# Block 0 of each feed-forward layer computed token-major, one tile of 128 tokens after the other

## The chip, the cores and the metric

One NeuronCore of a Trainium2 chip runs the whole program. The metric is device time in microseconds (us) of one launch; lower is better.

## The reference

Two small transformer stacks, two layers each, follow each other on one activation `x` of 256 tokens by 1024 features, batch 1, in fp32. Every layer ends in a gated feed-forward:

```python
x = x + swiglu(rmsnorm(x, norm_ffn[layer]), w_gate_up[layer], w_down[layer])    # first stack
h = rms_norm(x, ffn_norm[l])                                                      # second stack
x = x + (jax.nn.silu(h @ w_gate[l]) * (h @ w_up[l])) @ w_down[l]
```

Ahead of the four feed-forwards stand, in this order: a pooling mixer, a blockwise attention (called moba in the kernel), and twice a mixer of four attentions (called mix). The hidden width is 2816; each of the attention stages ends with an output projection whose product is added to `x`.

## The kernel before

**Precision by splitting.** Every large product is made of three: a weight is stored as `whi` (ACT copies `raw` to fp32r) plus `wlo` (DVE subtracts `whi` from `raw`), the activation as `h_hi` plus `h_lo`, and hi*hi, hi*lo and lo*hi are summed in PSUM. One **unit** is 1 MB of weights, 128 partitions by 2048. `split` on ACT makes `whi` (L619), `split` on DVE makes `wlo` (L904). There are 179 units in one fixed sequence, three slots each for `raw`, `whi` and `wlo`; a slot is free for ACT when PE has used unit n-3, and the load of a unit (SP, L412) waits until the low part of unit n-3 is made. The counters are semaphores: `hi_ready`, `lo_ready`, `units_used`.

**The order of work** is written out by hand for each engine; nothing is scheduled by a planner. Each engine executes its own list from top to bottom, and a wait stops all that stands behind it on that engine. The two attention stages are lists of events (`moba_script`, `mix_script`) that PE, ACT and DVE each walk through.

**Attention's end.** The output projection takes four units. `residual` (L1365 to L1367) multiplies one unit of 2 x 128 rows of weights into four accumulators, PSUM banks 4 to 7 (`ACC`): token tile t and column half h go to `ACC[2t+h]`, with 6 matmuls of 512 columns each, so 24 per unit. Before, each unit is done for both tiles before the next one begins.

**The norm.** For tile t, DVE adds each accumulator to `x` (`add_residual`, L914), ACT squares with a sum (L630), DVE adds up (L920), GpSimd (POOL) takes the power -0.5 (L568), DVE scales (`normalise`, L932), PE transposes eight 128x128 pieces (L1474, banks 0 to 3), ACT copies them as `h_hi` (L637) and DVE makes `h_lo` (L939). Before, DVE's `norm` does both tiles' adds first, and PE waits for all four halves ahead of block 0.

**The feed-forward** (`ffn(f)`, f = 0 to 3; its first unit is u0). The hidden width is cut into 11 blocks of 256; a block has three units, gate, up and down. Gate and up are computed feature-major: the weights stand still and the tokens stream, in two parts of 512 and 256 columns (`both_halves`, L1391 and L1395, 32 matmuls a unit). The two kinds of sum lie side by side in PSUM, and DVE adds them (`sum_gate`, L1029; `sum_up`, L1036). The first unit of block 0 is special, `first_both_halves` (L1406, L1407, L1410, then L1391 and L1395): it starts as soon as `h_hi` is there. Then ACT's silu (L669) and DVE's product and split (`glu`, L1044, L1051, L1053) give `o_hi` and `o_lo` for the down unit, which is done one block later. PE's order is gate 0, up 0, gate 1, up 1, down 0, gate 2, up 2, down 1 and so on. The end of a feed-forward is already computed by tile: the last two down units are done for tile 0 first, then for tile 1, and for f = 0 and f = 2 `residual` puts the eight transposes of the next norm's tile 0 between the halves of tile 1. The stage behind it then begins token-major (`first_token_major`, L1435, L1436, L1439), with tile 1's transposes between the tiles.

## Time and profile before

| | |
|---|---|
| median of 3 runs | 1178.37 us (1177.03 to 1178.8) |
| the profiled execution | 1178.07 us, of which its span 1176.0 us |
| matmuls (PE), DVE, ACT busy | 97%, 67%, 46% of the span |
| DMA | 205 MB, 174 GB/s, 54.4% of 16 engines' span |
| TensorE clock granted, mean | 0.991 of full |

The rows of a timeline give the start in us from the span's beginning, the length in us, engine, source line and operation, output and inputs; in square brackets, how long the engine sat idle before it and what released it. `x16` means sixteen in a row that were merged. Matmuls are pipelined: a row says 0.39 us for one, but the next one starts 0.23 us later, so rates are read from starts.

### The profile page before, as it was taken

How to read it: one execution, taken by the hardware profiler on the slowest of the kernel's cores; microseconds unless marked ns; L12 is line 12 of the kernel's file. 1: busy time of each engine (PE TensorE's matmuls, PEld its weight loads, DVE VectorE, ACT ScalarE, POOL GpSimd, SP SyncE). 2: the span in 40 equal slices, each digit the busy share in tenths (PEclk: the TensorE clock that was granted, in tenths of full speed). 3: DMA queues.
4: the chain of work that ended last, by engine and by line, in shares of the span. 5: the costliest groups of instructions: out<-in, count | busy, mean ns of one | idle time of the engine just before them, and what ended most of it. 6: DMA issues, size and time to landing. Idle time of an engine off the chain costs nothing.

```text
span 1176.0 us, 17176 instructions
## 1 busy us (share of the span) xinstructions
PE 1139.4 (97%) x6750; PEld 989.8 (84%) x6750; DVE 789.1 (67%) x997; ACT 535.5 (46%) x696; POOL 34.7 (3%) x47
## 2 busy tenths in 40 slices
PE   6899999999999999999999999999999999999997
PEld 4788888899878888889988788888898887888886
DVE  4776666856667666677676676666766766766665
ACT  4534333456654343344566433433446655333332
POOL 0000000000000000002100000000030000000000
PEclk9899999999999999999999999999999999999999
DMA  8565656673436556586432465565863234655560
GB/s 276 195 215 179 213 179 185 208 244 115 141 117 227 179 179 213 179 219 197 152 107 86 139 224 182 183 206 181 217 202 112 73 112 139 206 188 182 185 204 36
DMA packets 167672, 205.14 MB, mean 174 GB/s; under 512 B 19983, under 2 KB 150535, under 8 KB 167618
## 3 DMA queue, kind: packets, MB, share of 16 engines
q1 hardware_dynamic: 167618, 204.40, 54.4%
q8 instruction: 37, 0.61, 0.2%
q14 instruction: 17, 0.14, 0.0%
HBM read 203.22 MB, written 1.16 MB: 174 GB/s over the span
## 4 chain that ended last, share of the span: by engine, by line
PE 90%; DVE 3%; SPq 2%; ACT 1%; issue 1%; POOL 1%; DMA 0%; DVEq 0%; POOLq 0%; ACTq 0%
PE bank L1391 27%; PE bank L1395 14%; PE bank L1365 13%; PE bank L1366 13%; PE bank L1367 13%; PE bank L1582 3%; PE bank L1594 2%; PE bank L1474 1%; PE bank L1604 1%; ACT junk L630 1%; PE bank L1798 1%; DVE x L914 1%; PE bank L1741 1%; DVE xn L932 1%; POOL rstd L568 1%
## 5 line engine op out<-in xcount | busy, mean ns | idle before, releaser
L619 ACT ACTIVATE whi<-raw 128x2048 fp32r<-128x2048 f32 x177 | 338.6, 1914 | 413.7 <-PE bank L1395 271.0
L904 DVE TENSOR_TENSOR wlo<-raw,whi 128x2048 fp32r<-128x2048 f32 x176 | 403.5, 2294 | 162.4 <-ACT whi L619 162.3
L1391 PE MATMUL bank<-h_both,whi 128*128 128x512 f32 x1376 | 327.6, 390 | 0.0
L1391 PEld LDWEIGHTS bank<-h_both,whi 128*128 128x128 f32 x1376 | 255.0, 188 | 50.8
L1395 PEld LDWEIGHTS bank<-h_both,wlo 128*128 128x128 f32 x1376 | 176.7, 191 | 6.9
L1395 PE MATMUL bank<-h_both,wlo 128*128 128x256 f32 x1376 | 178.8, 283 | 0.0
L1365 PE MATMUL bank<-whi,o_hi 128*128 128x512 f32 x448 | 175.9, 393 | 0.6 <-DVE o_lo L1142 0.6
L1366 PE MATMUL bank<-wlo,o_hi 128*128 128x512 f32 x448 | 174.9, 390 | 0.0
L1367 PE MATMUL bank<-whi,o_lo 128*128 128x512 f32 x448 | 174.4, 389 | 0.0
L1365 PEld LDWEIGHTS bank<-whi,o_hi 128*128 128x128 f32 x448 | 84.3, 188 | 18.4 <-issue 2.3
L1367 PEld LDWEIGHTS bank<-whi,o_lo 128*128 128x128 f32 x448 | 84.1, 188 | 17.9
L1366 PEld LDWEIGHTS bank<-wlo,o_hi 128*128 128x128 f32 x448 | 84.3, 188 | 15.6
L1029 DVE TENSOR_REDUCE pr<-bank 128x512 f32<-128x1024 f32 x44 | 53.9, 1224 | 49.0 <-PE bank L1395 49.0
L1365 PE MATMUL bank<-h_both,whi 128*128 128x256 f32 x288 | 83.3, 289 | 0.0
L1366 PE MATMUL bank<-h_both,whi 128*128 128x256 f32 x288 | 81.5, 283 | 0.0
L1367 PE MATMUL bank<-h_both,wlo 128*128 128x256 f32 x288 | 81.4, 283 | 0.0
L1036 DVE TENSOR_REDUCE pr<-bank 128x512 f32<-128x1024 f32 x40 | 49.0, 1224 | 46.2 <-PE bank L1395 46.2
L703 ACT ACTIVATE pr<-pr,negmax 128x256 f32<-128x256 f32 (+1 forms) x96 | 46.0, 480 | 31.1 <-DVE negmax L1118 31.1
L1365 PEld LDWEIGHTS bank<-h_both,whi 128*128 128x128 f32 x288 | 55.1, 191 | 2.6 <-issue 2.3
L1366 PEld LDWEIGHTS bank<-h_both,whi 128*128 128x128 f32 x288 | 55.2, 192 | 0.1
L1367 PEld LDWEIGHTS bank<-h_both,wlo 128*128 128x128 f32 x288 | 55.2, 192 | 0.0
L1365 PE MATMUL bank<-whi,h_both 128*128 128x256 f32 x160 | 46.4, 290 | 1.5 <-DVE wlo L904 1.5
(165 smaller groups left out, 1144.2 us busy)
## 6 DMA issues: line engine op xcount, KB each, us to landing
raw<-in_w_gate_up SPq DMA_DIRECT2D x44, 1024.0 KB, 5.1
raw<-in_w_down SPq DMA_DIRECT2D x44, 1024.0 KB, 4.9
raw<-in_w_gate SPq DMA_DIRECT2D x22, 1024.0 KB, 5.3
raw<-in_w_up SPq DMA_DIRECT2D x22, 1024.0 KB, 5.3
raw<-in_w_in SPq DMA_DIRECT2D x20, 1024.0 KB, 6.3
raw<-in_w_o SPq DMA_DIRECT2D x12, 1024.0 KB, 5.0
raw<-in_w_kv SPq DMA_DIRECT2D x8, 1024.0 KB, 5.6
raw<-in_w_q SPq DMA_DIRECT2D x4, 1024.0 KB, 6.2
```

The costliest lines, as they stand in the source:

```text
L619: act.activation(whi[:, s, :], raw[:, s, :], ACT.Copy).then_inc(hi_ready, 1)
L703: e = act.activation(pr[:, s, q, 0:w], src, ACT.Exp, bias=negmax[:, s, q:q + 1], scale=-1.0 if biased else 1.0, accum_out=psumrow[:, s, q: ...
L904: dve.tensor_tensor(wlo[:, s, :], raw[:, s, :], whi[:, s, :].bitcast(F32), ALU.subtract).then_inc(lo_ready, 1)
L1029: dve.tensor_reduce(gate32, halves(ACC[0] if first else 0), AX_X, ALU.add).then_inc(gate_sum, 1)
L1036: dve.tensor_reduce(up32, halves(ACC[2] if first else 2), AX_X, ALU.add).then_inc(up_sum, 1)
L1365: pe.matmul(dst, ahi, bhi, start=first, stop=False)
L1366: pe.matmul(dst, ahi, blo, start=False, stop=False)
L1367: return pe.matmul(dst, alo, bhi, start=False, stop=last)
L1391: pe.matmul(bank[bk + jj][:, :], hi[:, kc, jj * P:(jj + 1) * P], h_both[:, kc, :, :].rearrange("p a t -> p (a t)"), start=(kc == 0), stop= ...
L1395: mm = pe.matmul(bank[bk + jj][:, T:2 * T], lo[:, kc, jj * P:(jj + 1) * P], h_hi[:, kc, :], start=False, stop=(kc == KC - 1))
L1582: mm = pe.matmul(bank[i % 2][:, qt * T:qt * T + w], q[:, qt * P:(qt + 1) * P], k[:, 0:w], start=True, stop=True)
L1594: mm = pe.transpose(bank[2 + q % 2][:, at:at + P], pr[:, i % 8, qt, kt * P:(kt + 1) * P], ident[:, :])
```

## The change

**PE.** The last two output units of moba and of both mix stages are done for tile 0, then for tile 1 (`last_two_by_tile`), with the eight transposes of tile 0 of the feed-forward's norm between the two halves of tile 1's last unit. Block 0's gate and up are computed token-major, 256 weight columns streaming past a standing tile of `h`: for tile 0 gate hi*hi and hi*lo, then lo*hi, then up hi*hi and lo*hi; then tile 1's transposes; then tile 1's gate, tile 0's missing third of up, and the rest. The weight split of up (`lo_ready` of u0+1) is needed only behind the norm of tile 1.

**ACT and DVE.** ACT makes `whi` of u0+1 between the squares of tile 0 and its copies instead of ahead of the norm. DVE normalises tile 0 ahead of the adds of tile 1, and splits u0+1 and u0+2 around tile 1's low parts. Block 0 has no `sum_gate` and `sum_up`; silu and the product are made in two token-major pieces of 128x256. Since the down unit wants features on the partitions, PE transposes the product with four 128x128 transposes behind the gate unit of block 1, ACT copies the result as `o_hi`, DVE makes `o_lo`. The first feed-forward has the same block 0 but follows the pooling mixer, whose end is unchanged.

The core of the diff (renumbered counters of `gate_sum` and `up_sum`, which lose one step per layer, are left out):

```diff
@@ the two event scripts @@
-    s += unit(14) + [("unit", 15), ("split", 17)]
+    s += unit(14) + [("unit", 15)]
...
-    s += V(14, 15) + [("O", 3)] + unit(13) + [("unit", 14), ("split", 16)]
+    s += V(14, 15) + [("O", 3)] + unit(13) + [("unit", 14)]
@@ ACT: norm and ffn @@
-            def norm(j, square_too=True, late_split=None):
+            def norm(j, square_too=True, late_split=None, by_tile=False):
+                by_tile = by_tile or late_split is not None
...
-                    if t == 0 and late_split is not None:
-                        split(late_split)
+                    if t == 0 and by_tile:
+                        if late_split is not None:
+                            split(late_split)
                         for h in range(2):
                             h_out(j, 0, h)
-                for t in range(0 if late_split is None else 1, TT):
+                for t in range(1 if by_tile else 0, TT):
...
-                norm([1, 4, 7, 9][f])
+                norm([1, 4, 7, 9][f], late_split=u0 + 1 if f else None, by_tile=True)
+                split(u0 + 2)
...
+                def first_silu(t):
+                    if t == 0:
+                        act.wait_ge(gate_up_tile0, f + 1)
...
+                    else:
+                        act.wait_ge(units_used, u0 + 2)
+                    i = act.activation(pr[:, 0, t, :], bank[ACC[t]][:, 0:FB], ACT.Silu)
+                    if t:
+                        i.then_inc(silu_ready, 1)
+                def first_act_hi():
+                    act.wait_ge(act_transposed, f + 1)
+                    act.activation(o_hi[:, 0:2, :], bank[ACC[2]][:, :].rearrange("p (c k) -> p c k", c=2), ACT.Copy).then_inc(act_hi, 1)
...
-                split(u0 + 2)
-                silu(0)
+                first_silu(0)
                 split(u0 + 3)
+                first_silu(1)
...
-                block_steps(1)
+                split(u0 + 1, 1)
+                first_act_hi()
+                split(u0 + 2, 1)
+                silu(1)
+                split(u0 + 3, 1)
@@ DVE: ffn @@
-                norm([1, 4, 7, 9][f])
+                add_residual(NORM_X[j], 0, 0)
+                add_residual(NORM_X[j], 0, 1)
+                mean_square(NORM_X[j], 0)
+                if f == 0:
+                    add_residual(NORM_X[j], 1, 0)
+                normalise(j, 0, 0)
+                normalise(j, 0, 1)
+                if f:
+                    add_residual(NORM_X[j], 1, 0)
+                h_lo_out(j, 0, 0)
+                add_residual(NORM_X[j], 1, 1)
+                h_lo_out(j, 0, 1)
+                mean_square(NORM_X[j], 1)
+                normalise(j, 1, 0)
+                normalise(j, 1, 1)
                 split(u0 + 1)
+                h_lo_out(j, 1, 0)
+                h_lo_out(j, 1, 1)
+                split(u0 + 2)
...
+                def first_glu():
+                    for t in range(TT):
+                        if t == 0:
+                            dve.wait_ge(silu_ready, e0 + 1)
+                        i = dve.tensor_tensor(pr[:, 1, t, :], pr[:, 0, t, :], bank[ACC[t]][:, FB:2 * FB], ALU.mult)
+                    i.then_inc(glu_ready, 1)
+                def first_act_lo():
+                    dve.wait_ge(act_hi, e0 + 1)
+                    dve.tensor_tensor(o_lo[:, 0:2, :], bank[ACC[2]][:, :].rearrange("p (c k) -> p c k", c=2),
+                                      o_hi[:, 0:2, :].bitcast(F32), ALU.subtract).then_inc(act_ready, 1)
...
-                split(u0 + 2)
-                sum_gate(0)
                 split(u0 + 3)
-                sum_up(0)
-                glu(0, 0)
+                first_glu()
...
-                block_steps(1, 1)
+                split(u0 + 1, 1)
+                first_act_lo()
+                sum_gate(1)
+                split(u0 + 2, 1)
+                sum_up(1)
+                glu(1, 1)
+                split(u0 + 3, 1)
@@ PE: helpers and ffn @@
+            def tile_pass(dst, t, h, w, first=False, last=False):
+                for kc in range(KC):
+                    mm = pe.matmul(dst, h[:, kc, tile(t)], w[:, kc, :], start=(first and kc == 0), stop=(last and kc == KC - 1))
+                return mm
+            def tile_hi(n, dst, t, j):
+                hi, lo = w8(n)
+                pe.wait_ge(lo_ready, n + 1)
+                for kc in range(KC):
+                    if kc % 4 == 0:
+                        pe.wait_ge(hT_hi, 4 * HT_NO[j] + 2 * t + kc // 4 + 1)
+                    pe.matmul(dst, h_hi[:, kc, tile(t)], hi[:, kc, :], start=(kc == 0), stop=False)
+                    pe.matmul(dst, h_hi[:, kc, tile(t)], lo[:, kc, :], start=False, stop=False)
+            def last_two_by_tile(n, chunks, ready, j):
+                for t in range(TT):
+                    for i in range(2):
+                        if t == 0:
+                            pe.wait_ge(lo_ready, n + i + 1)
+                            pe.wait_ge(out_lo, ready[i])
+                        mm = residual(n + i, chunks[i], O, False, i == 1, (t,), j if t and i else None)
+                        if t:
+                            used(mm)
...
-                for t in range(TT):
-                    transposes(j, t)
-                used(first_both_halves(u0, ACC[0], j))
+                    transposes(j, 0)
+                gate = [bank[ACC[t]][:, 0:FB] for t in range(TT)]
+                up = [bank[ACC[t]][:, FB:2 * FB] for t in range(TT)]
+                gate_hi, gate_lo = w8(u0)
+                up_hi, up_lo = w8(u0 + 1)
+                tile_hi(u0, gate[0], 0, j)
+                wait_h(j, 0)
+                tile_pass(gate[0], 0, h_lo, gate_hi, last=True)
+                pe.wait_ge(hi_ready, u0 + 2)
+                tile_pass(up[0], 0, h_hi, up_hi, first=True)
+                tile_pass(up[0], 0, h_lo, up_hi)
+                transposes(j, 1)
+                tile_hi(u0, gate[1], 1, j)
                 pe.wait_ge(lo_ready, u0 + 2)
-                used(both_halves(u0 + 1, ACC[2]))
+                tile_pass(up[0], 0, h_hi, up_lo, last=True).then_inc(gate_up_tile0, 1)
+                wait_h(j, 1)
+                used(tile_pass(gate[1], 1, h_lo, gate_hi, last=True))
+                tile_pass(up[1], 1, h_hi, up_hi, first=True)
+                tile_pass(up[1], 1, h_lo, up_hi)
+                used(tile_pass(up[1], 1, h_hi, up_lo, last=True))
+                def first_act_transposes():
+                    pe.wait_ge(glu_ready, e0 + 1)
+                    for jj in range(2):
+                        for t in range(TT):
+                            mm = pe.transpose(bank[ACC[2]][:, jj * T + t * P:jj * T + (t + 1) * P],
+                                              pr[:, 1, t, jj * P:(jj + 1) * P], ident[:, :])
+                    mm.then_inc(act_transposed, 1)
...
                         used(both_halves(u0 - 1 + u, 2 * u))
+                        if off == 1 and u == 0:
+                            first_act_transposes()
@@ PE: the output units of the two attention stages @@
-                        mm = residual(u, 2 * (n - 12), O, n == 12, n == 15)
+                        mm = residual(u, 2 * (n - 12), O, n == 12, False)
                         used(mm)
+                    elif n == 15:
+                        last_two_by_tile(u - 1, (4, 6), (3, 4), 4)
...
+                        elif n == 14:
+                            last_two_by_tile(u - 1, MIX_OUT_CHUNK[2:4], [OUT_LO[l][i] + 1 for i in (2, 3)], 7 + 2 * l)
```

**PE at the entry into the last feed-forward**, before (the last three matmuls are of the last output unit; `h_both` holds both parts of h):

```order
L1365 MATMUL bank<-whi,o_hi 128x512
L1366 MATMUL bank<-wlo,o_hi 128x512
L1367 MATMUL bank<-whi,o_lo 128x512
L1474 MATMUL bank<-ident,xn 128x128 x16
L1406 MATMUL bank<-h_both,whi 128x256
L1407 MATMUL bank<-h_both,wlo 128x256
...
L1410 MATMUL bank<-h_both,whi 128x256 x8
L1391 MATMUL bank<-h_both,whi 128x512 x8
L1395 MATMUL bank<-h_both,wlo 128x256 x8
```

and now, from the point where the last six output matmuls remain (the line numbers are those of the changed kernel):

```order
L1541 MATMUL bank<-ident,xn 128x128 x8
L1419 MATMUL bank<-whi,o_hi 128x512
L1420 MATMUL bank<-wlo,o_hi 128x512
...
L1495 MATMUL bank<-whi,h_both 128x256
L1496 MATMUL bank<-wlo,h_both 128x256
...
L1485 MATMUL bank<-whi,h_both 128x256 x24
L1541 MATMUL bank<-ident,xn 128x128 x8
L1495 MATMUL bank<-whi,h_both 128x256
L1496 MATMUL bank<-wlo,h_both 128x256
...
L1485 MATMUL bank<-wlo,h_both 128x256 x8
L1485 MATMUL bank<-whi,h_both 128x256 x24
L1485 MATMUL bank<-wlo,h_both 128x256 x8
```

Eight transposes now stand ahead of the last six output matmuls, and 40 matmuls of tile 0 (16 in L1495 and L1496, 24 in L1485) ahead of the other eight.

**DVE at the same entry**, before:

```order
L904 TENSOR_TENSOR wlo<-raw,whi 128x2048 [waits hi_ready]
L914 TENSOR_TENSOR x<-x,bank 128x512 [waits acc_ready] x2
L920 TENSOR_SCALAR msq<-ssq 128x1 [waits rstd_ready,squares]
L914 TENSOR_TENSOR x<-x,bank 128x512 [waits acc_ready]
L914 TENSOR_TENSOR x<-x,bank 128x512 [waits units_used]
L932 SCALAR_TENSOR_TENSOR xn<-x,rstd,gains 128x512 [waits xT_ready,rstd_ready,gains_in1]
```

and now:

```order
L928 TENSOR_TENSOR wlo<-raw,whi 128x2048 [waits hi_ready]
L938 TENSOR_TENSOR x<-x,bank 128x512 [waits acc_ready] x2
L944 TENSOR_SCALAR msq<-ssq 128x1 [waits rstd_ready,squares]
L956 SCALAR_TENSOR_TENSOR xn<-x,rstd,gains 128x512 [waits xT_ready,rstd_ready,gains_in1]
L956 SCALAR_TENSOR_TENSOR xn<-x,rstd,gains 128x512 [waits xT_ready,rstd_ready]
L938 TENSOR_TENSOR x<-x,bank 128x512 [waits acc_ready]
L963 TENSOR_TENSOR h_both<-bank,h_both 128x4x128 [waits hT_hi]
L938 TENSOR_TENSOR x<-x,bank 128x512 [waits units_used]
```

Tile 0 is scaled ahead of both adds of tile 1, and its first low part stands ahead of the last add.

## Rows read from the trace of the kernel before

**Rows 1.** The page, busy time: us, share of the span, instructions.
```profile
PE 1139.4 (97%) x6750; PEld 989.8 (84%) x6750; DVE 789.1 (67%) x997; ACT 535.5 (46%) x696; POOL 34.7 (3%) x47
```
**Rows 2.** PE's waits: us in total, times, longest.
```profile
PE bank L1474 <- DVE xn L932: 12.9, 14, 4.1
```
**Rows 3.** Timeline of PE at the entry into the last feed-forward (f = 3).
```profile
969.80 0.50 PE L1365 MATMUL bank<-whi,o_hi 128*128 128x512 f32 x1
...
980.63 0.39 PE L1367 MATMUL bank<-whi,o_lo 128*128 128x512 f32 x1
...
982.46 0.65 PE L1474 MATMUL bank<-ident,xn 128*128 128x128 f32 x4 [1.45 <-DVE xn L932]
...
984.66 1.97 PE L1474 MATMUL bank<-ident,xn 128*128 128x128 f32 x8 [0.54 <-DVE xn L932]
...
986.55 0.55 PE L1406 MATMUL bank<-h_both,whi 128*128 128x256 f32 x1
...
992.83 3.82 PE L1391 MATMUL bank<-h_both,whi 128*128 128x512 f32 x16
...
998.40 3.82 PE L1391 MATMUL bank<-h_both,whi 128*128 128x512 f32 x16
```
**Rows 4.** The same for f = 1 and f = 2: first output matmul, then block 1.
```profile
327.86 0.50 PE L1365 MATMUL bank<-whi,o_hi 128*128 128x512 f32 x1
...
356.55 1.32 PE L1391 MATMUL bank<-h_both,whi 128*128 128x512 f32 x5
...
651.21 0.50 PE L1365 MATMUL bank<-whi,o_hi 128*128 128x512 f32 x1
...
678.81 1.55 PE L1391 MATMUL bank<-h_both,whi 128*128 128x512 f32 x6
```
**Rows 5.** Stretches: length, busy us (count) of PE, PEld, DVE, ACT, POOL, PEclk, DMA.
```profile
664.80:666.80 2.00, 1.38 (x9) 0.91 (x10) 1.55 (x4) 0.99 (x3) 0.42 (x1) 1.00 0.00 0
986.50:988.00 1.50, 1.50 (x8) 1.48 (x8) 1.34 (x3) 1.33 (x2) 0.00 (x0) 0.58 0.00 0
```
**Rows 6.** Timeline of PE at the entry into the second mix stage.
```profile
849.25 1.32 PE L1474 MATMUL bank<-ident,xn 128*128 128x128 f32 x8 [0.44 <-DVE xn L932]
...
850.33 0.47 PE L1365 MATMUL bank<-whi,o_hi 128*128 128x512 f32 x1
...
851.79 0.28 PE L1435 MATMUL bank<-whi,h_both 128*128 128x256 f32 x1
...
853.71 1.12 PE L1439 MATMUL bank<-whi,h_both 128*128 128x256 f32 x8
...
855.15 1.32 PE L1474 MATMUL bank<-ident,xn 128*128 128x128 f32 x8 [0.32 <-DVE xn L932]
...
856.59 0.35 PE L1435 MATMUL bank<-whi,h_both 128*128 128x256 f32 x1
```
**Rows 7.** Timeline of the first mix stage: four transposes of probabilities among output matmuls.
```profile
644.12 0.42 PEld L1594 LDWEIGHTS bank<-ident,pr 128*128 128x128 f32 x4 [0.39 <-issue]
...
644.53 0.48 PE L1365 MATMUL bank<-whi,o_hi 128*128 128x512 f32 x1
```
**Rows 8.** Timeline of PE at the entry into the first feed-forward (f = 0).
```profile
34.01 4.31 PE L1474 MATMUL bank<-ident,xn 128*128 128x128 f32 x16 [4.14 <-DVE xn L932]
...
38.24 0.55 PE L1406 MATMUL bank<-h_both,whi 128*128 128x256 f32 x1
...
49.81 0.40 PE L1391 MATMUL bank<-h_both,whi 128*128 128x512 f32 x1
```
**Rows 9.** Stretches of the same entry.
```profile
36.00:38.20 2.20, 2.12 (x10) 1.57 (x8) 2.20 (x5) 1.20 (x2) 0.00 (x0) 0.50 0.00 0
39.00:40.40 1.40, 1.40 (x14) 1.40 (x14) 1.40 (x2) 0.00 (x0) 0.00 (x0) 1.00 0.00 0
```
**Rows 10.** The page's groups: the two splits, busy us, mean ns, idle before.
```profile
L619 ACT ACTIVATE whi<-raw 128x2048 fp32r<-128x2048 f32 x177 | 338.6, 1914 | 413.7 <-PE bank L1395 271.0
L904 DVE TENSOR_TENSOR wlo<-raw,whi 128x2048 fp32r<-128x2048 f32 x176 | 403.5, 2294 | 162.4 <-ACT whi L619 162.3
```

More of the change, by code:

```diff
@@ L1639, in _ @@
                         used(mm)
-                    else:
+                    elif n < 14:
                         if n == 12:
@@ L1707, in mix @@
                             used(mm)
-                        else:
+                        elif n < 13:
                             if n == 11:
@@ L1713, in mix @@
                             else:
[L1714 to L1715 removed]
+                                pe.wait_ge(out_lo, OUT_LO[l][1] + 1)
+                            mm = residual(u, MIX_OUT_CHUNK[n - 11], O, n == 11, False)
                             used(mm)
+                        elif n == 14:
+                            last_two_by_tile(u - 1, MIX_OUT_CHUNK[2:4], [OUT_LO[l][i] + 1 for i in (2, 3)], 7 + 2 * l)
                     elif k == "mla_T":
```

62 lines of the change are left out of this document (24 added, 38 removed).

## The prediction

> **What bounds the kernel now.** The page comes first: PE is busy 97% of the span, 1139.4 of 1176.0 us, no other engine over 67% [rows 1]. So a microsecond is worth something only where PE stands still or runs slowly, and all but 36.6 us of the span are already filled. The list of waits then says where it stands: 12.9 us over 14 waits go to transposes (L1474) that wait for the scaled `x` (DVE, L932) [rows 2]. This is the norm between two stages. The timeline of one such place shows the pattern. Ahead of the last feed-forward the last output matmul starts at 980.63; transposes start at 982.46, then in steps until 984.66, and block 0's first product at 986.55 [rows 3]. From the first matmul of the last two output units (969.80) to the gate unit of block 1 (998.40) it is 28.60 us. The same stretch takes 28.69 us at f = 1 (327.86 to 356.55) and 27.60 us at f = 2 (651.21 to 678.81) [rows 4]. The stretches with the granted clock explain the difference of a microsecond: at f = 3 it is 0.58 while block 0 begins, 0.50 being the lower level of 1.2 GHz; at f = 2 it stays at 1.00, which is 2.4 GHz [rows 5]. PE had stood and waited in both.
>
> **The new entry at f = 1, 2, 3.** The same pattern exists already where a feed-forward ends and a mix stage begins, so its durations are read there [rows 6].
> 1. The 48 output matmuls stay: 969.80 to 980.86 (0.23 us behind the last start), 11.06 us [rows 3]. Their order by tile costs nothing that the rows show, since the sums of the four accumulators are independent.
> 2. Eight transposes between them: 849.25 to 850.33, 1.08 us, and the six matmuls behind them take 1.46 us (to 851.79) instead of 6 x 0.23 = 1.38: together 1.16 [rows 6]. There PE had waited 0.44 us for DVE ahead of them. I take no wait: DVE there was late with the adds because it still had a split in hand (2.294 us each [rows 10]), and here the split of u0 ends before the first accumulator is done.
> 3. 40 matmuls of 256 columns for tile 0. The matmuls 851.79 to 853.71 are 16 in 1.92 us, 0.12 each [rows 6]: 4.80 us.
> 4. Tile 1's transposes and the gap behind them, 855.15 to 856.59: 1.44 us [rows 6]. Their data came 3.36 us after 851.79 there, against 4.80 us of cover here, so the wait of 0.32 us goes.
> 5. The other 56 matmuls: 6.72 us.
>
> Sum 25.18 us. Against 28.69, 27.60 and 28.60 that saves 3.51, 2.42 and 3.42, together 9.35 us. The arithmetic itself is equal: 96 x 0.12 = 11.52 us for what the two units of 32 matmuls do in the old form (5.57 us for one, 992.83 to 998.40 [rows 3], so 11.14). That +0.38 is inside the sum.
>
> A row shows that loading the standing operand is hidden: 16 matmuls, each with its own load, came at 0.12 us. The Trainium skill (TensorE: Matmul & The Clock Gate, Part 3, The mechanism) says LDWEIGHTS overlaps matmuls in flight "only when row_grp differs", and all matmuls here use all rows. By that rule the 32 more loads of a layer would lie on the path and the sum of an entry would be some 29.9 us instead of 25.18; the trace disagrees in the rows named, and the measurement decides.
>
> **f = 0.** The pooling mixer's end is not changed, only block 0. Sixteen transposes took 34.01 to 38.24, 0.26 each, with the clock at 0.50, and block 0's start too; from 39.0 it is 1.00 [rows 8, 9]. Before: 34.01 to 49.81, 15.80 us [rows 8]. Now: 8 transposes 2.1; 96 matmuls 11.5; 8 transposes 1.44; and of the matmuls some 13 (from 36.1 to 38.9) run at the lower level, where 256 columns take about twice 0.12, +1.3. That is 16.3, 0.5 longer, while the first transposes can start up to 0.4 us earlier, since DVE scales tile 0 before the second add of tile 1. I take -0.2 (a loss). The ends are -1.0 (clock as late as before and no earlier start) and +1.5 (the second tile's idle steps gone).
>
> **What is added.** Four transposes of the product in block 1. The nearest rows are four transposes among output matmuls, 644.12 (the first load of the four) to 644.53: 0.41 us, with 0.39 us idle ahead of them [rows 7]. That idle time was PE's own between two kinds of work. I take 0.41 and no idle, since the product is done in time (next paragraph): 4 x 0.41 = 1.64 us; with it, 3.2. Two `tensor_reduce` leave DVE per layer, and four small operations come; DVE stands idle 33% and ACT 54% of the time [rows 1], so this is costed at nothing as long as the margins below hold. The loads are the same in number and order; those of block 1 follow splits that move by about one split (2.294 us [rows 10]), and each is used more than a unit later.
>
> **What could be late next.** For the product: PE's last 24 matmuls of block 0 take 2.9 us. When they begin, ACT may split u0+3 (1.914 us) and then DVE (2.294) [rows 10]; that ends 1.3 us behind block 0. The second silu (256 columns) stands beside it, and the two products of 256 columns take some 0.3 us each at the rate of DVE's row (2.294 us for 2048), so with hand-overs the product is there about 2.5 us behind block 0, an estimate from these rows. PE asks for it 5.57 us behind block 0. The margin is about 3 us. For up's `wlo` (u0+1), DVE starts behind tile 1's scaling, about 4.0 us after tile 0's matmuls began (the data came at 3.36, plus half of that step), and ends at 6.3; PE asks at 4.80 + 1.44 + 16 x 0.12 = 8.2. Tile 1's low parts end about 7.7 and are asked at 9.1. Margin 1.4 to 1.9 us. At ACT, the split of u0+1 stands ahead of tile 0's copies and begins when the second-last unit is used, 6 matmuls before the transposes: 1.4 + 0.65 us of cover for 1.9 us.
>
> **Sum.** 9.35 - 0.2 - 1.64 = 7.5 us off. The profiled execution took 1178.07 us (span 1176.0 and 2.07 around it), 0.30 below the median of 1178.37. So 1170.6 for it, and 1170.9 against the median.
>
> **Rivals.**
> All times here stand against the median.
> *A, second-tile chain late (0.12).* The margins of 1.4 us are the sum of eight steps on four engines. If DVE or ACT comes 1.5 us after PE asks at each of the three entries, 4.5 us return: saving 3.0, time 1175.4. For: DVE's list puts the first low part ahead of the last add. Against: the rows of the mix entry, with the same list, show only 0.44 and 0.32 us of waiting [rows 6].
> *B, clock falls anyway (within the forecast's range).* If the granted clock still falls at f = 1 and 3, about 1 us each comes back: 1172.9. Against: at f = 2 even the old waits left it at 1.00 [rows 5].
> *C, the loads do not hide (0.02).* Block 0 then pays for 32 more loads of the standing operand in each layer. PEld has 989.8 us for 6750 loads, 0.147 each [rows 1]; 4 x 32 x 0.147 = 18.8 us: 1189.7. Against it stand the 0.12 us [rows 6]. The rule of the Trainium skill named above is the case for it.
> *D, slower by the new wait (0.04).* Place: the four transposes at the head of up 1 wait for `glu_ready`, and behind them stands all of PE. DVE has the split of u0+3 ahead of the product, ACT has the same split ahead of the second silu. It costs each microsecond by which the product comes later than 5.57 us behind block 0. To turn the sum beyond +2.4 us it must cost (7.5 + 2.4)/4 = 2.5 us in every layer, so the product would have to be 5.5 us later than worked out: two whole units. Time at that point: 1180.8 and above. Against: ACT and DVE have nothing else to do there.
> *E, no effect (0.04).* If out_lo or `wlo` of the last output unit comes too late for the new order (asked 12 matmuls, 2.75 us, after the second-last unit begins), tile 0's sums end no earlier and only the block's own overlap is left; saving about 1.5 us: 1176.9.
>
> **How the numbers follow.** The forecast has 0.78, A 0.12, E 0.04, D 0.04, C 0.02. A measurement of this kernel can tell about 0.2% from no change, 2.4 us. The forecast's own range is 7.5 us with +1.7 (f = 0) and +1 (small waits also gone) on one side, and -0.8 (f = 0), -1.6 (idle ahead of the four transposes) and -1.2 (clock or small waits) on the other: 1168.2 to 1174.5. The 8-in-10 range reaches a little into A: 1167.8 to 1174.8. Faster by over 0.2% has the forecast and most of A: 0.90. Within 0.2%: 0.05. Slower: 0.05.
>
> **What would show it.** Right: at f = 1, 2, 3 the stretch from the first of the last two output units to block 1's gate is about 25.2 us each, and 1.00 is granted in all three; waits of PE on `xn` fall from 12.9 us to about 6; four transposes in block 1 start without idle; f = 0 is unchanged within a microsecond. Wrong, if PE's waits name `wlo`, `h_both` or `pr` instead, if the 256-column matmuls of block 0 start over 0.12 us apart at full clock, or if the second-last output unit waits.

## The result, and the profile after

The changed kernel takes **1167.04 us**, median of four runs (1166.50 to 1169.28), the kernel before 1178.59 (four runs, 1177.03 to 1180.06). The ratio is 0.9908, 95% interval 0.9894 to 0.9923: 11.55 us faster. The prediction was 1170.9 us, range 1167.8 to 1174.8. The sign was right, and the time is 0.8 us below the range.

The profile after is of the execution of 1169.28 us, the slowest of the four and 2.24 us above their median. Its span is 1167.3 us, against 1176.0 before. The page, busy time, beside [rows 1]:

```profile
PE 1137.9 (97%) x6862; PEld 995.3 (85%) x6862; DVE 778.7 (67%) x989; ACT 536.7 (46%) x704; POOL 32.8 (3%) x47
```

PE has 112 matmuls more, 28 per layer: four transposes, and 96 matmuls for block 0's gate and up instead of 72. It is busy for 1.5 us less. DVE gave up 10.4 us, on an engine that did not bound the kernel.

PE's waits, beside [rows 2] (us in total, times, longest):

```profile
PE bank L1541 <- DVE xn L956: 5.3, 5, 3.5
...
PE bank L1495 <- DVE wlo L928: 1.0, 3, 0.3
...
PE bank L1495 <- ACT h_both L638: 0.3, 1, 0.3
```

The wait for the scaled `x` went from 12.9 us to 5.3, and 3.5 of these are one wait, at f = 0. At f = 1, 2 and 3 none is left for `xn`. What remains there is 0.34 us at tile 1's first matmul, put down to `wlo`. The copies of tile 1 by ACT stand in that gap too.

The timeline of PE at the entry into f = 3, beside [rows 3] (start, us, engine, line, operation, count, idle before):

```profile
964.30 0.50 PE L1419 MATMUL bank<-whi,o_hi 128*128 128x512 f32 x1
...
974.00 1.03 PE L1541 MATMUL bank<-ident,xn 128*128 128x128 f32 x8
974.79 0.48 PE L1419 MATMUL bank<-whi,o_hi 128*128 128x512 f32 x1
...
976.24 0.28 PE L1495 MATMUL bank<-whi,h_both 128*128 128x256 f32 x1
...
981.04 1.04 PE L1541 MATMUL bank<-ident,xn 128*128 128x128 f32 x8
982.41 0.36 PE L1495 MATMUL bank<-whi,h_both 128*128 128x256 f32 x1 [0.34 <-DVE wlo L928]
...
989.20 3.14 PE L1445 MATMUL bank<-h_both,whi 128*128 128x512 f32 x13
```

The eight transposes of tile 0 stand inside the output units and wait for nothing. From the first output matmul to block 1's gate it is 24.90 us (964.30 to 989.20). It is 24.86 at f = 1 (327.98 to 352.84) and 24.90 at f = 2 (647.96 to 672.86), against 28.60, 28.69 and 27.60 [rows 3, 4].

At f = 0, beside [rows 8]:

```profile
32.77 1.94 PE L1541 MATMUL bank<-ident,xn 128*128 128x128 f32 x8 [3.49 <-DVE xn L956]
...
41.32 1.03 PE L1541 MATMUL bank<-ident,xn 128*128 128x128 f32 x8
...
49.48 0.86 PE L1445 MATMUL bank<-h_both,whi 128*128 128x512 f32 x3
```

The pooling's last matmul starts at 29.01, so that entry takes 20.47 us. Before it took 20.22 (29.59 to 49.81).

The account from profile to profile closes (a stage is the stretch between two entries):

- Three entries: 3.83 + 2.70 + 3.70 = 10.23 us less.
- f = 0: 0.25 more.
- The four transposes: every stage behind an entry is about 0.45 us longer, 1.8 together. An example is 49.81 to 327.86 before, 278.05 us, and 49.48 to 327.98 now, 278.50 us.
- The pooling ends 0.58 us earlier (29.59 to 29.01), of which 0.43 us are the first transfer, which landed earlier (PE's first matmul at 9.74 us, before at 10.17). That is no part of the change.
- Sum: 10.23 - 0.25 - 1.80 + 0.58 = 8.76, and the spans, given to a tenth, differ by 8.7.

So the mechanism is there, but **8.7 us between two profiles is not 11.55 us between two medians**. The experiments had to find the rest. They also had to show which part of the change earns what.

### The profile page after: what moved, and what is told of

Its sections match the earlier page's. It is cut to its first block, busy times and chain, and to the rows that moved or that the text cites. A ratio compares the mean times of both kernels' runs of the same rounds, so it can differ in the third digit from the quotient of the medians.

```text
span 1167.3 us, 17434 instructions
## 1 busy us (share of the span) xinstructions
PE 1137.9 (97%) x6862; PEld 995.3 (85%) x6862; DVE 778.7 (67%) x989; ACT 536.7 (46%) x704; POOL 32.8 (3%) x47
## 4 chain that ended last, share of the span: by engine, by line
PE 90%; DVE 4%; SPq 2%; issue 2%; ACT 1%; POOL 1%; DMA 0%; DVEq 0%; POOLq 0%; ACTq 0%
PE bank L1445 25%; PE bank L1449 13%; PE bank L1419 13%; PE bank L1420 13%; PE bank L1421 13%; PE bank L1676 3%; PE bank L1485 2%; PE bank L1688 2%; PE bank L1541 1%; DVE wlo L928 1%; PE bank L1698 1%; ACT junk L631 1%; PE bank L1897 1%; PE bank L1840 1%; DVE xn L956 1%
## 5 line engine op out<-in xcount | busy, mean ns | idle before, releaser
L1445 PE MATMUL bank<-h_both,whi 128*128 128x512 f32 x1280 | 304.7, 390 | 0.0
L1445 PEld LDWEIGHTS bank<-h_both,whi 128*128 128x128 f32 x1280 | 237.4, 188 | 47.5
L1449 PEld LDWEIGHTS bank<-h_both,wlo 128*128 128x128 f32 x1280 | 164.1, 191 | 6.2
L1449 PE MATMUL bank<-h_both,wlo 128*128 128x256 f32 x1280 | 166.0, 283 | 0.0
L1421 PE MATMUL bank<-h_both,wlo 128*128 128x256 f32 x288 | 81.4, 283 | 0.0
L1083 DVE TENSOR_REDUCE pr<-bank 128x512 f32<-128x1024 f32 x40 | 49.0, 1224 | 47.6 <-PE bank L1449 47.6
L1088 DVE TENSOR_REDUCE pr<-bank 128x512 f32<-128x1024 f32 x36 | 44.1, 1225 | 45.6 <-PE bank L1449 45.6
L1419 PEld LDWEIGHTS bank<-h_both,whi 128*128 128x128 f32 x288 | 55.1, 191 | 2.6 <-issue 2.3
L1420 PEld LDWEIGHTS bank<-h_both,whi 128*128 128x128 f32 x288 | 55.2, 192 | 0.1
L1421 PEld LDWEIGHTS bank<-h_both,wlo 128*128 128x128 f32 x288 | 55.2, 192 | 0.0
```

The lines of the kernel that those rows point to most:

```text
L1083: dve.tensor_reduce(gate32, halves(0), AX_X, ALU.add).then_inc(gate_sum, 1)
L1088: dve.tensor_reduce(up32, halves(2), AX_X, ALU.add).then_inc(up_sum, 1)
L1419: pe.matmul(dst, ahi, bhi, start=first, stop=False)
L1420: pe.matmul(dst, ahi, blo, start=False, stop=False)
L1421: return pe.matmul(dst, alo, bhi, start=False, stop=last)
L1445: pe.matmul(bank[bk + jj][:, :], hi[:, kc, jj * P:(jj + 1) * P], h_both[:, kc, :, :].rearrange("p a t -> p (a t)"), start=(kc == 0), stop= ...
```

## Experiments

The theory (T1) was that the rest is TensorE's clock: the profiled execution had the lower level granted at the entry into the first feed-forward, where most executions have the full clock. The rival (T2) was other scatter, of the transfers at the start above all. Below, "entry" is the stretch from the first of the last two output units to block 1's gate (at f = 0 from the pooling's last matmul). Each group was timed beside the kernel before, whose medians on four chips were 1176.94, 1176.89, 1176.97 and 1177.35 us.

### Both kernels again

> The kernel before, unchanged: how far its own time moves from run to run, and with what clock. T1 (the missing 3 us are TensorE's clock at the first layer's entry, which was low in the one profiled execution after the change and is high in most others): profiles of this kernel whose granted clock is 0.991 have a span near 1176.0 us, and a higher clock goes with a shorter span. T2 (the rest is transfers at the start, or other scatter): spans move by 1 us or more at the same clock. Both: median 1178 to 1179 us, ratio 1.000.

> The changed kernel, unchanged. Both: median 1166.5 to 1167.5 us. T1: a profiled execution at a granted clock of 0.997 or 0.998 has a span of 1164.5 to 1165.5 us and its entry into the first layer (last matmul of the pooling to block 1's gate) takes 18 to 18.5 us instead of 20.47, while the entries of the three other layers stay at 24.9. T2: the entry into the first layer takes 20.4 us again and the difference is elsewhere.

> The changed kernel, unchanged, as the base of this group on its own chip. 1167 to 1168 us, runs between 1166.5 and 1169.5 us with clocks from 0.998 to 0.995; the ones above 1169 have 0.995 or 0.996. Its difference to the kernel before: 9.4 us if the earlier 11.55 us held 2 us of scatter between chips and days, 11.5 us if not.

Measured: before 1176.83 us (12 runs, 1175.15 to 1178.35), ratio 1.000 (0.9991 to 1.0008). After 1167.53 (6 runs, ratio 0.9924, 0.9910 to 0.9938), and on another chip 1167.37 (6 runs, 0.9919, 0.9906 to 0.9932). **The gain is 9.4 and 10.0 us there**, against 11.55 on the first chip. The changed kernel repeats within half a microsecond from chip to chip. It is the kernel before that moved, from 1178.6 to 1177. Two expectations were missed. For the kernel before 1178 to 1179 us was expected. For the entry at f = 0 it was 18 to 18.5 us, and 19.73 and 19.55 were measured: the clock still fell there, only for a shorter time. (One of the changed kernel's runs, 1170.13 us, is also above the 1169.5 us that was expected as the highest.)

Of the 16 runs of the changed kernel, three lie above 1169 us (1169.28, 1169.49, 1170.13), and these are the three with a mean granted clock of 0.995. The other 13 have 0.996 to 0.998 and lie between 1166.5 and 1168.8.

The difference between profiles has its place. This is the stage behind the second feed-forward, in the profile after, and in the second fence in that of the same kernel repeated, on another chip (length, busy us and count of PE, PEld, DVE, ACT, POOL, then PEclk, DMA share, GB/s):

```profile
532.00:534.00 2.00, 1.83 (x11) 1.39 (x12) 1.95 (x3) 1.19 (x3) 0.00 (x0) 0.93 0.00 0
534.00:536.00 2.00, 2.00 (x12) 2.00 (x11) 2.00 (x3) 1.80 (x2) 0.00 (x0) 0.50 0.00 0
536.00:538.00 2.00, 2.00 (x14) 2.00 (x14) 2.00 (x6) 0.00 (x0) 0.00 (x0) 0.72 0.13 24
```

```profile
532.00:534.00 2.00, 1.88 (x15) 1.56 (x14) 1.94 (x4) 1.79 (x3) 0.00 (x0) 1.00 0.00 0
534.00:536.00 2.00, 2.00 (x18) 1.80 (x16) 2.00 (x5) 1.21 (x1) 0.00 (x0) 1.00 0.00 0
536.00:538.00 2.00, 2.00 (x17) 2.00 (x17) 2.00 (x3) 1.93 (x5) 0.00 (x0) 1.00 0.36 76
```

The program is the same and so is what comes before: two waits of 1.4 us for a norm, which end at 526 and 532 us. In one execution the lower level is granted behind the second wait, in the other it is not. The stage is 295.12 us long in the first and 293.86 in the second: **1.26 us for one fall.** At f = 0 it is 20.47 us against 19.55, 0.92. Together 2.18, with 0.31 us on the other side where the pooling ends (29.01 and 29.32): 1.87, and the spans are 1.9 us apart (1167.3 and 1165.4). The change touches nothing near 534 us.

### What the falls cost either kernel: matmuls that nobody uses

```diff
+            def keep_busy(n):
+                for _ in range(n):
+                    pe.matmul(bank[2][:, :], h_hi[:, 0, 0:P], h_both[:, 0, :, :].rearrange("p a t -> p (a t)"), start=True, stop=True)
...
+                keep_busy(16 if f == 0 else 6)
```

This is for the kernel before. The changed one has `if f == 0: keep_busy(14)` at the same place, ahead of its transposes.

> The kernel before with extra matmuls, results unused, ahead of the transposes of each layer (16 at the first, 6 at each other). T1 with the clock low in before's ordinary executions and not in after's: about 2 us less at the first layer and 1 us less at the second and the fourth, median 1174 to 1176 us; the entries of layers 2 and 4 then take 27.6 us like layer 3 rather than 28.7 and 28.6. If the change's gain is all from waits and weight loads: 1178 us, and the stretches keep their length.

> The changed kernel with 14 extra 512-column matmuls, results unused, ahead of the first layer's norm (where TensorE waits anyway). T1: the entry into the first layer takes about 18 us at full clock in the profile, and the median stays within 0.5 us of the changed kernel's, 1166.5 to 1167.5 us, because most executions had the full clock already. If the clock is low there in ordinary executions too: 2 to 2.5 us below, about 1165 us. If it has nothing to do with the clock: no change in the stretch, 20.4 us.

Measured: the kernel before with them **1173.19 us** (8 runs, 1172.74 to 1174.14; ratio 0.9969, 0.9958 to 0.9980), 3.75 below the one without. Its entries take 19.43, 27.57, 27.61 and 27.60 us, and no stretch but the kernel's end is below 1.00. The waits for `xn` fell to 5.9 us, since the extra work fills them, but that alone saves nothing: the entry at f = 2 is 27.61 with them and 27.60 without. The gain came where the clock had fallen: 0.79 at f = 0, 1.12 at f = 1, 1.00 at f = 3, and 1.25 near 538 us, where no matmul was added. The changed kernel went to 1166.01 us (6 runs, 1165.64 to 1167.38), 1.5 less, and its first entry from 19.73 to 18.35. "1174 to 1176" was too high by a microsecond, and "within 0.5 us" too small by one: the clock is not high there in ordinary executions, contrary to T1.

With the falls at the entries gone in both the gain is therefore 1173.19 - 1166.01 = **7.2 us**. By the entries it is 1.08 + 3 x 2.70 - 1.80 = 7.4. The rest are falls of the clock: the kernel before has them at f = 1 and f = 3 (2.12 us) and the changed one has not; near 536 us (1.25) before has one in both its profiles and the changed kernel in one of three; at f = 0 the changed kernel loses more by it, 1.20 to 1.38 against 0.79. That gives 7.4 + 2.12 + 1.25 - 0.5 = 10.3 us, with 9.4 and 10.0 measured on the two chips.

### One half of the change alone

```diff
-                        mm = residual(u, 2 * (n - 12), O, n == 12, n == 15)
+                        mm = residual(u, 2 * (n - 12), O, n == 12, False)
...
+                    elif n == 15:
+                        last_two_by_tile(u - 1, (4, 6), (3, 4), 4)
...
-                for t in range(TT):
-                    transposes(j, t)
+                if f == 0:
+                    transposes(j, 0)
+                transposes(j, 1)
```

This is against the kernel before: the outputs, the norm and ACT's split in the new order, block 0 as it was. It is called the order alone below.

> The kernel before with one part of the change alone: the last two output units by tile with the first tile's transposes inside, the norm of tile 0 first, ScalarE's splits behind the norm of tile 1; block 0 stays in the old order, both tiles for each weight. Sum of the prediction: block 0's first matmul needs tile 1's transposes as before, so only the transposes' and their copies' wait goes: each of the three entries 27.6 to 28.3 us instead of 28.7, 27.6 and 28.6, 1 to 2 us less in all, median 1176.5 to 1177.5 us. Rival (the order of the outputs is what gains): 1170 us or less.

The other half, against the changed kernel. Only PE's outputs go back to the old order; the norm on DVE and ACT's splits keep the new one, so these stand in both runs:

```diff
-                    elif n == 15:
-                        last_two_by_tile(u - 1, (4, 6), (3, 4), 4)
+                    else:
...
+                        mm = residual(u, 2 * (n - 12), O, False, n == 15)
+                        used(mm)
+                        if n == 15:
+                            transposes(4, 0)
```

> The changed kernel with the last two output units back in the old order (both tiles for each unit), tile 0's transposes behind the last unit, block 0 by tile. Sum: tile 1's norm is hidden behind tile 0's 40 matmuls (4.8 us), but tile 0's norm chain is open: 1.8 to 2.5 us longer per entry than in the changed kernel, 26.7 to 27.4 us instead of 24.9, median 1172 to 1175 us. Rival (block 0's form carries all of the gain): 1167 us.

Block 0's form with the outputs in the old order: 1171.49 us (5 runs, 1171.04 to 1172.30; ratio 0.9953, 0.9937 to 0.9969), with entries of 26.18, 26.23 and 26.24 us. That is 0.5 us below the lower end of what was expected. **The order alone is slower than the kernel before: 1183.45 us** (6 runs, 1182.56 to 1185.73; ratio 1.0056, 1.0041 to 1.0072). Both the expectation and its rival named a gain, so both missed it, mine by its sign. Its waits, and one of them in its timeline at f = 1:

```profile
PE bank L1486 <- DVE xn L933: 18.8, 9, 3.8
```

```profile
340.46 1.03 PE L1486 MATMUL bank<-ident,xn 128*128 128x128 f32 x8
...
346.06 1.42 PE L1486 MATMUL bank<-ident,xn 128*128 128x128 f32 x8 [3.20 <-DVE xn L933]
```

In either order tile 1's sums end with the last output matmul. In the old one tile 0's transposes stood behind it and filled a part of the wait; now they stand ahead of it, so that it starts 11.69 us into the entry (342.48) and not 10.79 (338.65 in the kernel before). Tile 1's transposes follow 3.58 us behind it instead of 4.02, which takes back only half of that. The old block 0 asks for both tiles at its first weight, so PE waits 3.20 us at once, where it had waited 1.45, 0.35 and 0.54 in the old order. The lower clock follows: the entries take 29.36, 30.30 and 28.06 us, only the last with the clock at 1.00, and the first takes 24.09. To part the two costs the same kernel ran with extra matmuls ahead of the transposes (26 and 24 at f = 0, 24 elsewhere, 256 columns each, unused).

> The kernel with the order of the outputs and norm alone (1183.45 us), and with extra matmuls, results unused, in the waits for the norms, so that the clock stays high. Its entries took 28.06 us at full clock and 29.36 and 30.30 us with a fall, the first 24.1 us. If the clock is what makes it slower than the kernel before: entries of 28.0 us and a first one of 21 to 22 us, 1176 to 1178 us, and then compared with the kernel before with extra matmuls (1173.19 us) the order alone costs 3 to 4 us at full clock. If the wait itself is what costs: 1182 us or more.

Measured: 1176.79 us (11 runs, 1176.42 to 1177.57), entries 21.71, 28.00, 28.05 and 28.05. The clock was worth 6.7 us to it. Against the kernel before with extra matmuls (1173.19) it is 3.6 us slower, and that is the price at full clock: 2.28 at f = 0, three times 0.44 behind. At f = 0 the outputs are not touched, so the larger part, 2.28 us, belongs to the norm by tile ahead of the old block 0, and not to the outputs.

At full clock the parts combine like this, at f = 1 to 3, in us per entry. Only the first cell has the norm and ACT's splits in the old order; no run has them alone:

| | outputs by unit | outputs by tile |
|---|---|---|
| block 0, both tiles for each weight | 27.6 | 28.0 |
| block 0, tile by tile | 26.2 | 24.9 |

The order costs 0.4 with the old block; the outputs by tile earn 1.3 with the new one. Neither half is the change.

### Prices and margins of the changed kernel

```diff
-                    for jj in range(2):
+                    for jj in (0, 1, 0, 1, 0, 1):
```

> The changed kernel with the four transposes of block 0's product done three times (the repeats' results are the same): 8 more per layer, 32 in all. At the 0.11 us that transposes side by side take: 3.5 us more, 1170.5 us. At the 0.40 to 0.46 us per layer of four that the changed kernel grew by: twice that per layer, 3.6 us more. If there is a copy or a wait behind each set: 6 us or more. Extrapolated back it gives the price of the four that the change adds (1.64 us predicted, 1.86 us measured profile to profile).

Measured: 1170.92 us (6 runs, 1170.13 to 1171.71), 3.4 above 1167.53. In the profile each stage with eight more transposes is 0.83 to 0.90 us longer: **0.11 us each, 0.44 for the four that the change adds**, and PE is not idle ahead of any of them.

```diff
+                split(u0 + 1)
                 mean_square(NORM_X[j], 1)
                 normalise(j, 1, 0)
                 normalise(j, 1, 1)
-                split(u0 + 1)
```

> The changed kernel with VectorE's half of the split of block 1's activation weights ahead of the squares of the second tile, instead of behind its norm. The second tile's norm is 2.3 us later; TensorE has 1.37 us of transposes and copies there and waited 0.3 to 1.4 us for VectorE in the profile, so nearly all of it shows: 1.5 to 2.3 us longer per entry, 4.5 to 9 us in all, 1171.5 to 1176 us. Rival (40 matmuls cover it): 1167 us, no change.

Measured: 1169.07 us (6 runs, 1168.10 to 1170.06), about 1.5 above, where 1171.5 to 1176 was expected. Entries take 25.42, 25.46 and 25.46 us, 0.55 longer, where 1.5 to 2.3 was expected. The profile names tile 1's norm again, but for 0.34 us:

```profile
980.07 1.32 PE L1541 MATMUL bank<-ident,xn 128*128 128x128 f32 x8 [0.34 <-DVE xn L956]
```

VectorE scales tile 1 16.43 us into the entry (979.26) instead of 14.51 (977.02 in the changed kernel repeated), 1.92 us later, and PE's transposes start 17.24 us into it instead of 16.74, 0.50 later. So tile 0's 40 matmuls had 1.4 us of slack. That is the 4.80 - 3.36 = 1.44 us of the prediction; the expectation of this run had left it out.

```diff
-                norm([1, 4, 7, 9][f], late_split=u0 + 1 if f else None, by_tile=True)
+                norm([1, 4, 7, 9][f], by_tile=True)
...
-    s += unit(14) + [("unit", 15)]
+    s += unit(14) + [("unit", 15), ("split", 17)]
```

(and the same in the mix script.)

> The changed kernel with ScalarE's first half of the split of block 1's activation weights back in its old place, ahead of the norm, for the three layers behind attention. ScalarE's split (1.9 us) then waits for the third and fourth output unit's weights to be used, or runs between the outputs, and the squares of tile 0 stand behind it. If it stands behind the last output unit's matmuls: tile 0's transposes come 3 to 4.5 us later per entry and the three entries take 28 to 29 us, time 1177 to 1181 us. If the split runs early enough: 1167.5 us, no change, and the edit of ScalarE's order was not needed.

Measured: **1185.61 us** (5 runs, 1184.94 to 1186.44; ratio 1.0075, 1.0061 to 1.0089), 18 us above the changed kernel, slower than the one before and beyond the 1177 to 1181 us that was expected. Entries: 30.72, 30.62 and 31.69 us. ScalarE's timeline at f = 3 shows why, with PE's first transposes in the second fence:

```profile
982.40 1.91 ACT L620 ACTIVATE whi<-raw 128x2048 fp32r<-128x2048 f32 x1 [6.04 <-PE bank L1421]
984.22 0.61 ACT L631 ACTIVATE junk<-x 128x512 bf16<-128x512 f32 x1
```

```profile
987.54 1.97 PE L1541 MATMUL bank<-ident,xn 128*128 128x128 f32 x8 [3.88 <-DVE xn L956]
```

The split writes a buffer that PE gives back when it has used a unit. By tile, the last two units are given back only in tile 1's pass (`if t: used(mm)`), so a split that used to start between the units now waits 6.04 us, and the squares of tile 0 stand behind it. **The new order of the outputs on PE makes the new place of the split on ScalarE compulsory**; it is the most expensive line of the change, and my account had it as a detail. The clock then falls in all three entries as well, and its share of the 18 us was not measured apart.

### A version that is faster

In the changed kernel only f = 0 keeps ScalarE's split ahead of the squares of tile 0. This moves it behind, as at the other layers:

```diff
-                norm([1, 4, 7, 9][f], late_split=u0 + 1 if f else None, by_tile=True)
+                norm([1, 4, 7, 9][f], late_split=u0 + 1, by_tile=True)
...
-            split(2)
```

> A candidate: the changed kernel with ScalarE's split of the first layer's second weight also moved behind tile 0 of the norm, as the change does for the other layers; in the profile that split (28.06, 1.91 us) stands right ahead of the squares of tile 0, whose norm TensorE waits for 3.5 to 3.9 us. The norm starts up to 1.3 us earlier: 1 to 1.5 us less, 1166.0 to 1166.5 us; and if the clock then stays high there, as with the extra matmuls (18.35 us for the stretch instead of 19.7 to 20.5), 1165 us. Rival: the split of the second weight is then late, no change, 1167.5 us.

> The candidate (ScalarE's split of the first layer's second weight behind tile 0 of the norm), beside the changed kernel on one chip: 1165.6 us, 1.5 to 2.2 us below the changed kernel, with the ratio's interval apart from it.

Measured: 1165.64 us (5 runs, 1165.01 to 1167.64; ratio 0.9911, 0.9897 to 0.9925) and, beside the changed kernel's 1167.37 on one chip, **1164.94 us** (4 runs, 1163.99 to 1165.27; ratio to the kernel before 0.9892, 0.9878 to 0.9906; the changed kernel's was 0.9919, 0.9906 to 0.9932). The two intervals just touch, but no run of one lies within the other's. PE's wait at f = 0 is 2.1 us instead of 3.5 to 3.9, and the entry takes 18.13 and 17.94 us:

```profile
31.25 1.33 PE L1540 MATMUL bank<-ident,xn 128*128 128x128 f32 x8 [2.08 <-DVE xn L955]
```

In the old place the split also waited for its own transfer, and the squares behind it with it: in the changed kernel repeated it starts at 28.06 us, when the transfer has landed. Now the squares of tile 0 start at 27.82 and 27.27 us, 0.72 us behind DVE's first add. The clock still falls: 0.50 is granted from 32 to 34 us in the second of these profiles.

> The same candidate with extra matmuls whose results are unused: 10 at the first layer's entry and 5 ahead of each of the two waits for the norm in the attention stage at 525 and 531 us, where the clock fell in some profiles and not in others. If the clock explains the scatter: no low clock outside the end of the kernel, clock 0.999, runs within 1 us of each other, and 1164.5 to 1165.5 us. Rival (the scatter comes from elsewhere): runs 2.5 us apart as in the changed kernel, median as the candidate's.

> The changed kernel with unused extra matmuls in the first layer's entry (14) and in the two waits for the norm at 525 and 531 us, in the stage between the second and the third layer (6 each, 1.4 us): this is where the profile after had a half clock at 534 to 538 us and the repeated one had none, with the stage 295.12 us long against 293.84. If the clock's falls at these two places are the scatter: every run 1165.3 to 1166.3 us, none 2 us above another, stage 293.8 us in the profile. If the scatter comes from elsewhere (the transfers at the start): runs 1.5 to 2 us apart, as with extra matmuls at the first layer alone (1165.64 to 1167.38).

> The candidate with the extra matmuls at the first layer (10) and in the two right waits, at 525 and 531 us, instead of in the first attention stage, where the run before had them and they cost 1.5 us (its stage took 280.05 us against 278.54). 1.5 us less than that run: 1164.3 to 1164.8 us, clock 0.999, first entry 16.8 us.

The first of these put its second set of extra matmuls into the wrong stage, the one behind the first layer. That stage became 1.5 us longer (280.05 for 278.54), and the kernel took 1166.07 us (4 runs, 1165.53 to 1166.64), no faster than the candidate without. In the right place (`keep_busy(6)` ahead of each half's transposes in the stage behind the second layer) the candidate takes **1164.11 us** (4 runs, 1163.90 to 1164.28; ratio 0.9887, 0.9873 to 0.9901), 3.3 below the changed kernel, its first entry 16.82 us. The changed kernel with extra matmuls at the first layer (14) and there takes 1165.87 (4 runs, 1165.57 to 1166.78). Neither profile has a low clock outside the kernel's end. The spread of four runs is 1.2 and 0.4 us, where the changed kernel on that chip had 3.5 over six (1166.60 to 1170.13). That agrees with the clock as the source of the scatter, though four runs could miss a fall that comes in one of five.

T2 holds a part as well. In the changed kernel with extra matmuls in both places the first entry takes 19.08 us at full clock, against 18.35 with those at the first layer alone. The difference is the transfer that ScalarE's split waits for there:

```profile
28.52 1.92 ACT L620 ACTIVATE whi<-raw 128x2048 fp32r<-128x2048 f32 x1 [4.24 <-DMA raw<-in_w_gate_up]
```

The split starts 0.60 us ahead of the pooling's last matmul (29.12), in the other run 1.33 us ahead of it (27.38 and 28.71), so the norm comes 0.73 us later. From the first transposes to block 1's gate both take 14.44 us at full clock; the repeated profiles take 15.59 and 15.55 there, and the first one 16.71. A fall at f = 0 thus cost 1.1 us in the repeated profiles and 2.3 in the first; the entries of 20.47 and 19.55 us are closer together because the norm came 0.24 us earlier in the first. Besides, the pooling's last matmul starts between 28.34 and 29.59 us in the profiles, following the first transfer (PE's first matmul 9.03 to 10.17): 1.2 us of scatter in which the clock has no part.

## Why the prediction was right in its sign and low in its size

**The entries at f = 1, 2, 3: right, about 0.3 us each too long.** Predicted 25.18, measured 24.86 to 24.90, which together saves 10.23 instead of 9.35. The mis-sized term is step 2, the first tile's transposes: "1.08 us, and the six matmuls behind them take 1.46" was read from a place where PE had waited 0.44 us ahead of them [rows 6]. Without a wait the eight took 0.79 (974.00 to 974.79) and the six 1.45. Step 4 measured 1.37 for 1.44, step 5 6.79 for 6.72. Step 3 was exact: 4.80 us (976.24 to 981.04), 40 matmuls with a weight load each at 0.12. So rival C falls, and with it, for this kernel, the rule of the Trainium skill (TensorE: Matmul & The Clock Gate, Part 3, The mechanism) that the prediction weighed.

**f = 0: right in the profile, wrong for the median.** A loss of 0.2 was predicted and 0.25 measured. But the executions repeated at 19.55 and 19.73 us gain 0.6 against the kernel before (20.22, and 20.32 repeated). The lower level ended at about 37 us there, and in the profiled execution at about 38.8.

**The four transposes: right.** Predicted 1.64, measured 1.80 from profile to profile and 0.44 x 4 = 1.76 by the run with twelve of them. No idle time, as taken. Rival D did not happen, and the product was there in time: PE's waits name no `pr` at L1621. (The distance that D needed, 5.5 us, is one unit of 5.57 us and not the two that the prediction says.)

**One sign of being wrong appeared, without weight.** PE's waits name `wlo` (1.0 us, three times) and `h_both` (0.3 us, once) at L1495. These are the gaps of about 0.34 us between tile 1's transposes and its first matmul; step 4 had such a gap in its 1.44 us, and measured 1.37.

**The step that failed: "So 1170.6 for it, and 1170.9 against the median."** The sum carried one execution's difference over to the medians with an offset of 0.30 us. In that execution the clock had fallen in four places ahead of the kernel's end (32 to 39, 343 to 346, 537 to 541 and 984 to 988 us). I took back those at f = 1 and 3 and left the two others in, as if the changed kernel had them in every execution. It has both in the profile of 1169.28 us, and in its two others only a shorter one at f = 0. The place at 536 us lay outside the change, so the prediction never looked at it, and it is worth 1.25 us. The way from the forecast to the median: 1170.6 - 0.88 (entries) - 0.58 (start) + 0.21 (f = 0 and the transposes cost 0.05 and 0.16 more) = 1169.4, against 1169.28 for the profiled execution; 1.26 and 0.92 less for the two falls give 1167.2, against 1167.04. The range failed for the same reason: it held the scatter of the terms, and none of the executions. A part of the 11.55 us is no gain of the change either: beside the kernel before on two other chips it was 9.4 and 10.0 us. That the gain without the falls, 7.2 us, is near the 7.5 us forecast is luck: the 7.5 holds 2.1 us of falls taken back at f = 1 and 3, and has the three entries 0.9 us and f = 0 1.3 us too long (1.08 us gained there at full clock, a loss of 0.2 forecast).

**Rivals.** A (second tile late) did not happen; the run with the norm 1.9 us later shows the slack. B (the clock falls anyway) did not happen in any of the profiles of the unchanged changed kernel at f = 1, 2 or 3. It did at f = 1 and 2 of the order alone, with a wait of 3.20 us, and at all three with ScalarE's split early, with 3.9 us; at f = 3 of the order alone the same 3.20 us left it at 1.00. E fell with the stretches. The prediction gave ScalarE's split one sentence and no price; left in its old place it would have waited for the units given back by tile, and the kernel would have been 18 us slower.

## What to carry to other kernels

Measure the halves of a change apart before you credit one: here the new order with the old block 0 was 6.6 us slower than the kernel before, the new block 0 with the old outputs 5.4 faster, and the whole 9.4 to 11.5. When a loop is reordered so that a buffer is given back later, look on the other engines for whatever takes that buffer and stands ahead of critical work. And a forecast against a median needs the falls of the clock in the profile read over the whole span, not at the change alone: each can be a microsecond that the next execution does not have.

## What the runs showed of the hardware

- The same instructions with the same idle time ahead get the lower clock in one execution and not in the next: near 534 us in the changed kernel's first profile and in neither of its two others. Where a fall costs anything, it is 0.8 to 1.3 us here, and 2.3 for the longer one at f = 0 of the changed kernel's first profile.
- What a fall costs depends on the wait behind it. In both profiles of the kernel before and in the changed kernel's first it lies behind the second of the two waits near 534 us, and the stage is 1.2 to 1.3 us longer (294.66, 294.65 and 295.12 us, against 293.42 and 293.86 without a fall). In the order alone, with ACT's split early, and in the changed kernel with extra matmuls at f = 0 it lies behind the first wait. There it costs nothing (293.41, 293.85 and 293.86 us), for the second wait, 1.4 us elsewhere, is gone from the profile. The other ten profiles without work put there have no fall at this place; the runs don't show why.
- At the lower level matmuls of 256 columns start 0.21 us apart instead of 0.12 (34.99 to 36.06 at f = 0: five in 1.07), so less than twice as long.
- Work that is thrown away makes a kernel faster: 3.75 us in the kernel before for 34 unused matmuls in time that PE had idle anyway.
